# One-hot selectors swapped between ScalarE and VectorE, a dot in every gate group, and the second table's odd chunks requested from ScalarE's queue

## What is computed

```python
q = (hb @ w_q).reshape(TOKEN_BLOCK, PEER_HEADS, 2, PEER_DKEY // 2)
s = jnp.einsum('thpd,hpkd->thpk', q, sub_keys)
top_s, top_i = lax.top_k(s, PEER_TOPK)
...
best_s, best_pos = lax.top_k(cand_s, PEER_TOPK)
expert = jnp.take_along_axis(cand_i, best_pos, axis=-1)
g = jax.nn.softmax(best_s, axis=-1)
act = jax.nn.gelu(jnp.einsum('thkd,td->thk', u_tab[expert], hb))
wgt = g.astype(act.dtype) * act
return jnp.einsum('thk,thkd->td', wgt, v_tab[expert])
```

## Time and profile before

| | us |
|---|---|
| median of 3 runs | 977.26 |
| the profiled execution's own time | 976.05 |
| its span | 974.3 |
| PE busy | 911.8 (94%) |
| DVE busy | 553.6 (57%) |
| ACT busy | 259.6 (27%) |
| POOL busy | 253.9 (26%) |
| gate groups, from the first gate matmul to the first matmul of the second table | 516.48 to 648.60 |
| second table, first to last matmul | 648.60 to 960.1 |

### The profile page before, as it was taken

One profiled execution on the slowest core, in us unless ns is written; L12 is line 12 of the kernel. 1 busy time (PEld: TensorE's weight loads), 2 busy tenths in 40 slices (PEclk: granted clock), 3 DMA queues, 4 the chain that ended last, 5 costly groups with the idle time before them and its releaser, 6 DMA issues.

```text
span 974.3 us, 17939 instructions
## 1 busy us (share of the span) xinstructions
PE 911.8 (94%) x6850; PEld 839.1 (86%) x6850; DVE 553.6 (57%) x1155; ACT 259.6 (27%) x568; POOL 253.9 (26%) x239
## 2 busy tenths in 40 slices
PE   5799998889999999999998999999999999999996
PEld 3697997568898999998988999999998888888895
DVE  1455115757189949874547787784445454444523
ACT  2443233744534111112216666630000000000002
POOL 0000000410323053365441111138343333333200
PEclk9598999899999999999999999999999999999999
DMA  9664675033254689999999867679999999999981
GB/s 367 276 253 174 211 273 208 2 126 134 87 186 162 236 314 410 410 409 410 409 409 409 293 226 248 238 260 399 408 408 408 410 409 409 409 409 409 409 346 44
DMA packets 73984, 292.74 MB, mean 300 GB/s; under 512 B 9026, under 2 KB 9154, under 8 KB 67396
## 3 DMA queue, kind: packets, MB, share of 16 engines
q1 hardware_dynamic: 45508, 191.13, 50.6%
q0 software_dynamic: 28416, 100.78, 27.1%
HBM read 290.72 MB, written 1.05 MB: 299 GB/s over the span
## 4 chain that ended last, share of the span: by engine, by line
PE 48%; DMA 26%; ACT 2%; DVE 2%; issue 2%; POOL 1%; SPq 0%; DVEq 0%; ACTq 0%
PE bank L830 23%; DMA stage<-in_peer_v 20%; PE bank L886 12%; PE bank L839 4%; DMA A<-in_peer_u,row_expert 3%; DMA stage<-in_peer_u_t 2%; PE bank L573 1%; PE bank L574 1%; PE bank L575 1%; PE bank L727 1%; PE bank L724 1%; PE bank L726 1%; PE bank L779 1%; PE bank L757 1%; PE bank L699 1%
## 5 line engine op out<-in xcount | busy, mean ns | idle before, releaser
L886 PE MATMUL bank<-A,stage 128*128 128x160 f32 x2048 | 300.4, 303 | 11.1 <-DMA stage<-in_peer_v 2.7
L886 PEld LDWEIGHTS bank<-A,stage 128*128 128x128 f32 x2048 | 280.4, 190 | 31.0 <-DMA stage<-in_peer_v 29.3
L830 PE MATMUL bank<-A,stage 128*128 128x160 f32 x2048 | 289.2, 300 | 4.0 <-issue 2.3
L830 PEld LDWEIGHTS bank<-A,stage 128*128 128x128 f32 x2048 | 280.1, 190 | 7.4 <-issue 7.0
L1341 DVE SCALAR_TENSOR_TENSOR sum<-A,row_gate,sum 128x1024 f32<-128x1024 f32 x81 | 104.0, 1284 | 106.1 <-DMA A<-in_peer_v,row_expert 106.1
L1622 POOL DMA_INDIRECT A<-in_peer_u,row_expert x80 | 90.3, 1129 | 179.3 <-DVE row_dot L1328 167.0
L1328 DVE CUSTOM_DVE_ANT_0 A<-A 128x1024 f32<-128x1024 f32 x80 | 97.0, 1221 | 55.5 <-DMA A<-in_peer_u,row_expert 39.9
L1622 POOL DMA_INDIRECT A<-in_peer_v,row_expert x84 | 80.3, 956 | 133.0 <-DVE sum L1341 118.3
L1161 ACT ACTIVATE A<-bank 128x480 f32<-128x480 f32 x1 | 0.6, 571 | 273.8 <-PE bank L886 273.8
L575 PE MATMUL bank<-h_hi,ring_low 128*128 128x256 f32 x256 | 72.7, 284 | 0.0
L1108 ACT ACTIVATE A<-bank 128x160 f32 (+1 forms) x88 | 26.7, 304 | 160.0 <-PE bank L830 142.3
(11 more groups left out here) (234 smaller groups left out, 1243.6 us busy)
## 6 DMA issues: line engine op xcount, KB each, us to landing
stage<-in_peer_u_t SPq DMA_DIRECT2D x128, 512.0 KB
stage<-in_peer_v SPq DMA_DIRECT2D x128, 512.0 KB
A<-in_ada_w SPq DMA_DIRECT2D x24, 1024.0 KB, 7.5
A<-in_w_in SPq DMA_DIRECT2D x11, 1024.0 KB, 4.8
A<-in_w_q SPq DMA_DIRECT2D x8, 1024.0 KB, 5.3
A<-in_w_out SPq DMA_DIRECT2D x4, 1024.0 KB, 6.8
stage<-in_bias_mask SPq DMA_DIRECT2D x1, 2048.0 KB, 12.3
A<-in_peer_v,row_expert POOLq DMA_INDIRECT x84
```

Source lines behind the costliest of these rows:

```text
L830: mm = pe.matmul(o, stage[j][:, k * P:(k + 1) * P], H2[:, k, 0:ND], start=(k == 0), stop=(k == KD - 1))
L886: mm = pe.matmul(bank[b][:, n * ND:(n + 1) * ND], stage[c % SLOTS][:, m * P:(m + 1) * P], A3[:, c, :], start=(c == 0 and n == 0), stop=(c ...
```

## The change

- `ONE2`, with the gate in it, is now made on ScalarE (`one2_squares`, `one2_rest`): four Squares as before, then four Relus of 128 elements, each with two per-partition operands: `relu(gate - gate * square)`, with bias = gate and scale = minus gate. `less_gate` (minus gate) is a new tile in the space of `csil`, filled by one more VectorE instruction per token block.
- `ONE1`, without the gate, is now made on VectorE by one tensor_tensor over 4 x 128 elements, both operands broadcast (`one1`).
- `row()` is called in every gate group but the first, and `LATE` is 39: 57 dots before the groups, 39 in them, none after.
- Of chunks 8 to 127 of the second table SP requests only the even ones. ScalarE requests the odd ones, in a loop behind the GELU of the dots.

```diff
-LATE = 38
+LATE = GROUPS - 1
...
+        less_gate = csil[:, :, :].rearrange("p k v -> p (k v)")[:, 0:ND]
...
             with sp.Fori(1, CHUNKS // SLOTS) as i:
-                for j in range(SLOTS):
+                for j in range(0, SLOTS, 2):
                     sp.wait_ge(v_read, i * SLOTS + (j + 1 - SLOTS))
                     sp.dma_start(stage[j], v_rows[i * SLOTS + j]).then_inc(stage_full[j], 16)
...
-            pe.wait_ge(choice_t_ready, 2 * TB)
+            pe.wait_ge(choice_t_ready, 3 * TB)
...
-            def one1_squares(j, g, reused=True):
+            def one2_squares(j, g, reused=True):
 
                 if reused:
                     act.wait_ge(gates_done, g - 1)
                 for t in range(GT):
-                    last = act.activation(ONE1[:, j % 2, t, :], iota, ACT.Square,
+                    last = act.activation(ONE2[:, j % 2, t, :], iota, ACT.Square,
                                           bias=choice_t[:, 0, bass.ds(g * GT + t, 1)])
-                last.then_inc(one1_square, 1)
-
-            def one1_rest(j, g):
-                act.wait_ge(one1_square, g + 1)
-                act.activation(ONE1[:, j % 2], ONE1[:, j % 2], ACT.Relu, bias=1.0, scale=-1.0).then_inc(one1_made, 1)
+                last.then_inc(one2_square, 1)
+
+            def one2_rest(j, g):
+                act.wait_ge(one2_square, g + 1)
+                for t in range(GT):
+                    last = act.activation(ONE2[:, j % 2, t, :], ONE2[:, j % 2, t, :], ACT.Relu,
+                                          bias=choice_t[:, 2, bass.ds(g * GT + t, 1)],
+                                          scale=less_gate[:, bass.ds(g * GT + t, 1)])
+                last.then_inc(one2_made, 1)
...
+            with act.Fori(1, CHUNKS // SLOTS) as i:
+                for j in range(1, SLOTS, 2):
+                    act.wait_ge(v_read, i * SLOTS + (j + 1 - SLOTS))
+                    act.dma_start(stage[j], v_rows[i * SLOTS + j]).then_inc(stage_full[j], 16)
...
+                dve.tensor_scalar(less_gate[:, tt], bank[6 + tb][:, 2 * P:2 * P + n], -1.0, None, ALU.mult)\
+                   .then_inc(choice_t_ready, 1)
...
-            def one2(j, g):
-
-                for t in range(GT):
-                    tt = g * GT + t
-                    last = dve.tensor_scalar(ONE2[:, j % 2, t, :], iota, choice_t[:, 1, bass.ds(tt, 1)],
-                                             choice_t[:, 2, bass.ds(tt, 1)], ALU.is_equal, ALU.mult)
-                last.then_inc(one2_made, 1)
+            def one1(j, g):
+
+                dve.tensor_tensor(ONE1[:, j % 2, :, :], iota.unsqueeze(1).broadcast_to([P, GT, NK]),
+                                  choice_t[:, 1, g * GT:(g + 1) * GT].unsqueeze(2).broadcast_to([P, GT, NK]),
+                                  ALU.is_equal).then_inc(one1_made, 1)
...
-                if g % 2 == 1:
+                if g:
                     row()
```

More of the change, by code:

```diff
@@ L461, in build @@
         folded, act_out, dve_out = sem("folded"), sem("act_out"), sem("dve_out")
-        ones_made, multiplied, one1_square = map(sem, ("ones_made", "multiplied", "one1_square"))
+        ones_made, multiplied, one2_square = map(sem, ("ones_made", "multiplied", "one2_square"))
         topk_step, shifted, exped, choice_ready, scratch_free, turned, choice_t_ready = map(
@@ L857, in _ @@
                 for n in range(3):
-                    mm = pe.transpose(bank[6 + tb][:, n * P:(n + 1) * P], choice[:, (1, 0, 2)[n], tb, :], ident)
+                    mm = pe.transpose(bank[6 + tb][:, n * P:(n + 1) * P], choice[:, n, tb, :], ident)
                 mm.then_inc(turned, 1)
@@ L1140, in _ @@
                     gelu_chunk(j, i * SLOTS + j)
-            act.wait_ge(choice_t_ready, 2 * TB)
+            act.wait_ge(choice_t_ready, 3 * TB)
             for j in range(SLOTS):
-                one1_squares(j, j, reused=j >= 2)
-                one1_rest(j, j)
+                one2_squares(j, j, reused=j >= 2)
+                one2_rest(j, j)
                 if j:
@@ L1147, in gate_steps @@
             def gate_steps(i, j):
-                one1_squares(j, i * SLOTS + j)
-                one1_rest(j, i * SLOTS + j)
+                one2_squares(j, i * SLOTS + j)
+                one2_rest(j, i * SLOTS + j)
                 gelu_beside((j - 1) % SLOTS, i * SLOTS + (j - 1))
@@ L1545, in multiply @@
                    .then_inc(multiplied, 1)
-            dve.wait_ge(choice_t_ready, 2 * TB)
+            dve.wait_ge(choice_t_ready, 3 * TB)
             dve.wait_ge(ones_made, 2)
@@ L1552, in _ @@
                     dve.wait_ge(gates_done, g - 1)
-                one2(g, g)
+                one1(g, g)
                 if g:
```

## The result

The changed kernel takes **950.98 us** (median of 4 runs, 950.61 to 952.36), the kernel before 977.91 beside it. The ratio is 0.9722 (95% interval 0.9700 to 0.9744): 27 us faster. Forecast were 945.5 us and a range of 934 to 959. One edited line stands in no cut of the diff: TensorE's transposes of the choices now put the other index into place 0 of `choice_t`, so the Squares, which read place 0, now serve `ONE2`.

The account below looks back on a forecast made before the run. Bound: TensorE, its chunks late in the second table (DMA shared one to one with gathers), its own work and late selectors in the gate groups. 976.05 + 0.9 + 0 - 32.5 = 944.5; predicted 945.5 us, range 934 to 959.

Parts of the forecast that it names:

- The second table: Third queue gives chunks up to 2/3 of DMA; TensorE runs unhindered, 279 us in place of 311.5: -32.5.
- The gathers' end: In the second table's stage, gathers were to end at 268 us, ahead of TensorE's 279.
- Rival 2: Second table: the gathers end last and TensorE waits for the last sums; 949 to 955 us, chance 5%.
- Rival 1: Second table: the third queue gives no third share, chunks still get half; 967 us (963 to 972), chance 13%.
- The gate groups: ScalarE's chain was to keep a group at 3.30 us, gain 0 (from -7 to +13.5).
- 0.24 + 1.30 + R + 3.45: Time of two gate groups: Squares' start, Relus' start, four Relus (R = 1.60 us), then chunk's end; 6.59 us.
- no clock term enters: TensorE's clock was taken at its full level, 2.4 GHz, in the gate groups and second table.
- the case's own range: Whole kernel if the forecast case holds: 936 (cheap Relus, -7) to 953 us; the case has 74%.
- a DMA rate near 377 GB/s in the groups: Expected sign in the profile after: gate groups' DMA moving 95 loads, 122 us of 132.
- The start of the groups: ScalarE's chain now decides when TensorE starts the first gate group: 517.4 in place of 516.48, +0.9 us.
- The dots: A dot in every gate group is covered by TensorE; the 18 made behind the groups become none.

Follow-up runs that it names:

- one_queue: The changed kernel with all chunks of the second table requested by SP again: 976.16 us, ratio 0.9956.
- all_on_act: The changed kernel with chunks 8 to 127 all requested by ScalarE, none by SP: 977.21 us, ratio 0.9965.
- dots_only: The kernel before with a dot in every gate group but the first (39 in them), nothing else changed: 973.48 us, ratio 0.9944.
- queue_only: The kernel before with the odd chunks requested by ScalarE behind the GELU of the dots, nothing else changed: 980.13 us, ratio 0.9994.
- queue_early: The kernel before with odd chunks requested by ScalarE, the first eight requests moved ahead of the GELU of the dots: 977.33 us, ratio 0.9964.
- old_selectors: The changed kernel with the selectors made as before (ScalarE the plain one, VectorE the one with the gate): 945.41 us, ratio 0.9672.
- dot_first: old_selectors with VectorE's dot ahead of multiply in the gate groups: 935.7 us, ratio 0.9567.
- swap_dot_first: The changed kernel with VectorE's dot ahead of multiply, nothing else changed: 951.38 us, ratio 0.9729.

## Why the prediction was right, and where it was off

**The second table** was right in mechanism and size: chunks 2.18 us apart, no wait, 278.6 us against the 279 forecast, on the reading that queues share DMA equally. one_queue and all_on_act show that the number of queues does it. The even split is shown for two queues (51.3% and 51.1%); with three the shares were 42.5, 30.0 and 29.8%, as the chunks had all they could use. The Trainium skill, "DMA: Bandwidth & Descriptors", Queues, rings and completion order (each DMA engine goes round the queue rows that have work) agrees with these runs; its sentence under Issuing engines are not separate DMA queues, that a second issuing engine saves only the time of initiating, does not hold here: 2.3% hang on it.

**The gathers' end** was put 268 us into the stage, 10 ahead of TensorE. It came at 278.6, level with it. DMA moved 400 x 278.6 = 111.4 MB in the stage, 212.6 loads, where I had 208. It was not full all the time, as I had taken it: 334 GB/s in the first 10.4 us and 298 in the last 16, where the last sums ran one by one, 1.39 us each (929.38 to 936.2), on VectorE. Rival 2's mechanism was thus nearer than its 5% said, though it did not decide: TensorE's wait for the last sum was 0.33 us.

**Rival 1's price**, 967 us, was too low: its case is one_queue, by its ratio 0.9956 x 977.9 = 973.6. The stage there is 306 us where I had 300; the moved dots are worth half of what I gave them.

**The gate groups** were forecast at 132 us (3.30 a group, no gain and no loss) and took 137.4. The terms that were mis-sized are in "0.24 + 1.30 + R + 3.45": the Relus start 1.42 us behind the Squares, not the 1.30 that was measured before them for a Relu without operands, and R was 1.65 us for 1.60. That makes 0.24 + 1.42 + 1.65 + 3.45 = 6.76, which is the pair's time on the timeline to the hundredth; 20 pairs cost 3.4 us more. The rest is mostly the first group. TensorE had waited 3.42 us for it, and its clock fell to half for a while:

```profile
520.25 1.83 PE L840 MATMUL bank<-gate_buf 128*128 128x128 f32 x8 [3.42 <-ACT gate_buf L1131]
521.87 3.34 PE L831 MATMUL bank<-A,stage 128*128 128x160 f32 x16
525.04 1.05 PE L840 MATMUL bank<-gate_buf 128*128 128x128 f32 x8
```

Busy times, clock (third from the end), DMA share and GB/s in that group, and in the same place of the kernel before:

```profile
520.20:525.10 4.90, 4.86 (x25) 4.88 (x26) 0.69 (x1) 2.72 (x8) 0.00 (x0) 0.65 1.03 410
```

```profile
516.40:521.00 4.60, 4.52 (x36) 4.55 (x37) 2.18 (x6) 2.81 (x10) 0.00 (x0) 1.00 1.03 411
```

4.79 us for this group (520.25 to 525.04), where the kernel before needed 3.14 (516.48 to 519.62). That no clock term enters was wrong by this 1.65 us. It is no pure effect of the change: dots_only lost the same 1.65 us behind a wait as short as that of the kernel before.

The lower end of the case's own range, 936, does not follow from its sum: 945.5 - 7 is 938.5. It made no difference, as the groups came out on the dear side. One sign did not come: a DMA rate near 377 GB/s in the groups. It was 323 (44.4 MB, 85 loads; 42 for chunks and 42 gathers, where I had 48 and 47). I had counted the loads made ahead at the end of the stage and not taken off those already made ahead at its start; that this is the whole difference is not shown.

**The start of the groups**, forecast 0.9 later, came 3.8 later. 2.0 of that arose before the first table, where the two programs are alike; I count it as scatter: in ten profiles (before, after, and the first eight kernels above) the unchanged stretch up to the first chunk ended between 313.5 and 315.8. From there to the groups it was 202.7 to 206.1 us, in no order by selector (both ends with the old ones; the two longest, 204.9 and 206.1, are queue_only and queue_early, where TensorE waited 6.7 and 7.7 us for VectorE, which was still at its last dots). The 0.9 itself shows when it is counted from the GELU of chunk 87, behind which the Squares start. Before and after:

```profile
514.10 0.30 ACT L1108 ACTIVATE A<-bank 128x160 f32 x1 [2.26 <-PE bank L830]
```

```profile
516.96 0.30 ACT L1109 ACTIVATE A<-bank 128x160 f32 x1 [1.87 <-PE bank L831]
```

From there to the first gate matmul it was 2.38 us before (to 516.48) and is 3.29 now (to 520.25): +0.91, as forecast. The other 0.9 of the 1.8 arose in the first table's chunks.

**The dots** in every group cost nothing in the groups, as forecast, and `one1` took 0.69 us. In spans: forecast was 974.3 + 0.9 - 32.5 = 942.7, measured 950.5; of these 7.8 us the groups are 5.2, the start and what lies before it 2.9, the second table -0.4. Against the medians the gap is smaller, 5.5 us, because the changed kernel's profiled execution lay above the median of its runs where that of the kernel before lay below.

## What to carry to other kernels

When two streams starve each other on DMA, as here, count the queues, not the engines: the stream that the bound waits for gets a larger part by being requested on a second queue, at the other stream's cost. Then ask at once when the other stream ends: here the queue alone gave 0.1% to 0.4%, and 3.3% only after work of the other stream had been moved to a stage with DMA to spare. A batch on one engine is not cheaper if its partner splits on another: the swap of selectors took 0.65 us from VectorE's chain, which held a pair of groups at 6.62 us, and put 1.14 onto ScalarE's (1.65 for 0.63, and 0.12 of later start), which then held it at 6.76. What shortened the groups was the order of work, the dot ahead of `multiply`: 6.14.

## What the hardware showed that I had not expected

- **TensorE's clock after a wait.** Behind a wait of 2.51 us the first gate matmuls ran at full speed in three kernels (the kernel before, old_selectors, dot_first) and at half speed in a fourth, dots_only, where the granted clock from 518.96 to 523.75 was 0.64. Behind 3.42 us they ran slower in the changed kernel (0.65 from 520.2 to 525.1), and so they did in each of the seven other kernels that waited 3.25 to 7.7 us there. So the length of the wait alone does not tell. At the end of queue_only and queue_early, behind waits of 10.4 and 26.7 us, the fold's matmuls took 1061 and 1057 ns against 592 in the others, and the fold 3.6 us (959.70 to 963.33) for 1.9. Half speed is the lower of the clock's two levels, 1.2 for 2.4 GHz.
- **A per-partition operand costs more than its 92 ns**: with one operand the first Relu also started 0.1 us later behind its wait for the Squares (1.40 for 1.30 us), with two 0.12.
- **GpSimd's instruction for a gather** took 935 ns in the groups of old_selectors and 1147 ns in those of the changed kernel, at the same number of dots. It is not `one1` as such: swap_dot_first has `one1` too, and 936 ns. In the changed kernel the gather starts inside `one1` (578.09, `one1` from 577.73 to 578.42), in swap_dot_first ahead of it (581.54, `one1` from 582.01). It cost nothing here, as GpSimd had time.
